# Split first-block weights in the arena, and two units of the second block ahead of the second tile, in a four-sublayer decoder trunk

## The chip, the cores and the metric

One core of one Trainium2 chip runs the whole program. The metric is the device time of one execution in microseconds (us), lower is better.

## The reference

A trunk of two layers over x of 256 tokens by 1024 channels, all in float32. Each layer has a token mixer and then an MLP, so there are four sub-layers, numbered v = 0 to 3 below. Each is normed, modulated and gated, with shift, scale and gate computed from a conditioning vector c:

```python
def trunk(x, c):
    c_act = silu(c)
    for i in range(2):
        sh1, sc1, g1, sh2, sc2, g2 = split(c_act @ ada_w[i] + ada_b[i], 6)
        h = rms_norm(x, norm_mix_g[i]) * (1 + sc1) + sh1
        y = gla_mixer(h) if i == 0 else moba_mixer(h, positions)
        x = x + g1 * y
        h = rms_norm(x, norm_mlp_g[i]) * (1 + sc2) + sh2
        x = x + g2 * (square(relu(h @ mlp_w1[i])) @ mlp_w2[i])    # 1024 -> 4096 -> 1024
    return x
```

v = 0 is gated linear attention (chunks of 64 tokens, 4 heads), v = 2 is block-sparse softmax attention (8 heads of 128, QK norm and rotary on q and k; with 256 tokens there is one block, so it is plain causal attention), v = 1 and 3 are the MLPs.

## The kernel before

**Weights.** Every weight matrix is read from memory once, in units of 128 partitions x 1024 values (two row groups of 128 by 512 columns). SP loads two units with one DMA of 1 MB into one of 4 slots of `w_raw`. A product in float32 is made of three matmuls in fp32r: ACT writes the rounded high part of a unit to `w_hi` (`hi`, L985), DVE writes the remainder to `w_lo` (`lo`, L1342), and PE adds hi x hi, hi x lo and lo x hi (`three`, L479 to L481). `w_hi` and `w_lo` have 4 slots each, so `hi` of unit u waits until PE has finished unit u - 4 (`unit_used`). A slot of `w_raw` is loaded again when `lo` of both its units is done (`lo_made`). Activations are split in the same way: `a_hi` (L1052) on ACT, `a_lo` (L1493) on DVE.

**Blocks.** Four units are a block, 1024 rows by 512 columns. Tokens are in two tiles (tb = 0, 1) of 128. In a token-major block (`project`, `project_tiles`) the activations are the stationary operand and the weights stream 512 columns: 6 matmuls for a unit and a tile. In a channel-major block of an MLP (`up`, L638 to L640) the weights are stationary and 256 tokens stream: 24 matmuls for a unit. Each MLP has 8 pairs of blocks: the hidden block j (up) and its product with w2 (`down`). Hidden block 0 is token-major and is then turned by 8 transposes (`turn`, L623). Hidden blocks 1 to 7 are channel-major, and PE works on hidden block j + 1 before `down` of block j.

**Between two sub-layers.** The last product of a sub-layer ends with tile 0 ahead of tile 1. For each tile: DVE adds the gated result to x (`residual`, L1504 and L1505, two halves of 512 columns), ACT takes squares and the root (`squares`, L1007 to L1015), DVE scales (`scaled`, L1415 to L1419, writes `xn`), PE transposes `xn` (`turn_norm`, L569), and then in four quarters ACT modulates (L1048) and writes `a_hi` (L1052), and DVE writes `a_lo` (L1493). PE needs quarter u of a tile for unit u. The transposes of tile 0 stand before the last unit of the product before; those of tile 1 stand after the four tile-0 units of the next block 0 (`project_tiles`), and then come the four tile-1 units. `norm(v)`, on ACT and on DVE, holds this work in a fixed order, with `hi` and `lo` of the block's own four units in between. The order on every engine is written out by hand; an engine waits in order.

**The block-sparse stage** (v = 2) has 6 input blocks n (k, q, k, q, v, v) and 2 output blocks. On ACT `stats(n)` reads the result of block n out of PSUM (L1095) and takes squares per head (L1192). On DVE `cosines`, `rotate` and `scale` (L1641 to L1667) turn and norm it, one after each of the first three units of block n + 1. PE transposes the result (`turn_rot(n)`, L846) after the first unit of block n + 2. `tables()` (L1817, L1818) makes the rotary tables from `gains`, and `gate1()` adds the last gates (PE L560, DVE L1396).

**ada.** The modulation weights come by the queue of POOL (L359), 1 MB each. `ada()` on DVE multiplies them in (L1357, L1360, two instructions of 128 x 1024), at hand-placed points of the stages up to the first MLP, and twice plus twice at the start of the second.

**The arena** is one buffer of 14.5 K values per partition that the stages share by hand: `xn` at 0, `hT` at 2 K, relu and squares from 4 K to 6 K, the products of attention above.

## Time and profile before

| | us |
|---|---|
| median of 3 runs | 658.9 (656.29 to 660.45) |
| the profiled execution: its own time | 658.67 |
| its span, first to last instruction | 656.9 |
| PE busy in the span | 619.4 (94%) |
| PE weight loads busy | 517.4 (79%) |
| DVE busy | 474.5 (72%) |
| ACT busy | 340.7 (52%) |

The span is what the trace shows; 1.8 us of the execution's own time lie around it. Times of rows count from the start of the span. Matmuls overlap, and the end of each is modelled, so the distance from one matmul's start to the next says more than its duration, and PE counts as busy over very short gaps.

### The profile page before, as it was taken

What the parts mean: (1) busy time and instruction counts of PE and PEld (TensorE: products, weight loads), DVE (VectorE), ACT (ScalarE), POOL (GpSimd) and SP (SyncE); (2) the same over time, 40 slices, a digit from 0 to 9 for tenths busy, and PEclk for the clock granted to TensorE, in tenths of its full rate; (3) what the DMA queues carried; (4) which work ended last, traced back from release to release, by engine and by line L of the source; (5) the groups of instructions that cost most, each with busy time, mean ns of one, the idle gap of its engine ahead of it and who ended that gap; (6) DMA issues with size and microseconds to landing.
All of it is one profiled execution on the core that took longest, in us unless ns stands there. A gap on an engine that the chain in (4) does not pass through costs nothing.

```text
span 656.9 us, 9237 instructions
## 1 busy us (share of the span) xinstructions
PE 619.4 (94%) x3471; PEld 517.4 (79%) x3471; DVE 474.5 (72%) x660; ACT 340.7 (52%) x581; POOL 39.4 (6%) x65
## 2 busy tenths in 40 slices
PE   3699999898999999999997999999799999999997
PEld 2467865676889998998865778788598999899985
DVE  4648997987778978889866987865787654555465
ACT  3446633547755344435548677564875443554440
POOL 3030021000000110101100000000000000000000
PEclk9799999999999999999998999999999999999999
DMA  8999599574588998999955545344357555555501
GB/s 289 387 364 389 166 362 383 215 254 155 175 312 323 378 360 314 340 366 354 341 222 187 175 151 188 133 129 129 128 180 274 188 192 192 192 192 192 192 0 64
DMA packets 58797, 156.44 MB, mean 238 GB/s; under 512 B 2786, under 2 KB 3280, under 8 KB 58768
## 3 DMA queue, kind: packets, MB, share of 16 engines
q1 hardware_dynamic: 47008, 112.41, 48.5%
q0 software_dynamic: 11760, 43.67, 18.6%
q8 instruction: 16, 0.26, 0.2%
q14 instruction: 13, 0.11, 0.0%
HBM read 155.02 MB, written 1.05 MB: 238 GB/s over the span
## 4 chain that ended last, share of the span: by engine, by line
PE 71%; DVE 10%; ACT 7%; issue 3%; ACTq 0%; DVEq 0%
PE ps L479 14%; PE ps L481 13%; PE ps L480 13%; PE ps L640 8%; PE ps L639 8%; PE ps L638 8%; DVE w_lo L1342 2%; ACT arena L1048 2%; ACT w_hi L985 1%; DVE ada_acc L1360 1%; ACT arena L1007 1%; PE ps L560 1%; DVE arena L1419 1%; ACT arena L1192 1%; DVE x L1505 1%
## 5 line engine op out<-in xcount | busy, mean ns | idle before, releaser
L1342 DVE TENSOR_TENSOR w_lo<-w_raw,w_hi 128x1024 fp32r<-128x1024 f32 x192 | 232.8, 1222 | 122.5 <-ACT w_hi L985 122.1
L985 ACT ACTIVATE w_hi<-w_raw 128x1024 fp32r<-128x1024 f32 x192 | 201.8, 1058 | 226.7 <-PE ps L481 119.6
L479 PE MATMUL ps<-w_hi,a_hi 128*128 128x512 f32 x288 | 120.2, 417 | 16.0 <-DVE a_lo L1493 14.3
L638 PE MATMUL ps<-a_hi,w_hi 128*128 128x256 f32 x448 | 126.9, 283 | 0.0
L640 PE MATMUL ps<-a_hi,w_lo 128*128 128x256 f32 x448 | 126.8, 283 | 0.0
L639 PE MATMUL ps<-a_lo,w_hi 128*128 128x256 f32 x448 | 126.7, 283 | 0.0
L481 PE MATMUL ps<-w_hi,a_lo 128*128 128x512 f32 x288 | 114.1, 396 | 0.0
L480 PE MATMUL ps<-w_lo,a_hi 128*128 128x512 f32 x288 | 113.7, 395 | 0.0
L479 PE MATMUL ps<-w_hi,m_hi 128*128 128x512 f32 x256 | 100.1, 391 | 0.0
L480 PE MATMUL ps<-w_lo,m_hi 128*128 128x512 f32 x256 | 99.8, 390 | 0.0
L481 PE MATMUL ps<-w_hi,m_lo 128*128 128x512 f32 x256 | 99.6, 389 | 0.0
L639 PEld LDWEIGHTS ps<-a_lo,w_hi 128*128 128x128 f32 x448 | 85.9, 192 | 0.6
L638 PEld LDWEIGHTS ps<-a_hi,w_hi 128*128 128x128 f32 x448 | 85.9, 192 | 0.5
L640 PEld LDWEIGHTS ps<-a_hi,w_lo 128*128 128x128 f32 x448 | 85.9, 192 | 0.0
L479 PEld LDWEIGHTS ps<-w_hi,a_hi 128*128 128x128 f32 x288 | 55.0, 191 | 38.2 <-issue 12.4
L1360 DVE SCALAR_TENSOR_TENSOR ada_acc<-ada_raw,c_act,ada_acc 128x1024 f32<-128x1024 f32 x56 | 71.7, 1281 | 2.9 <-DMA ada_raw<-in_ada_w_dram 1.7
L481 PEld LDWEIGHTS ps<-w_hi,a_lo 128*128 128x128 f32 x288 | 54.9, 191 | 12.2
L480 PEld LDWEIGHTS ps<-w_lo,a_hi 128*128 128x128 f32 x288 | 55.2, 192 | 10.4 <-issue 0.2
L479 PEld LDWEIGHTS ps<-w_hi,m_hi 128*128 128x128 f32 x256 | 48.1, 188 | 11.0 <-DVE w_lo L1342 0.8
L481 PEld LDWEIGHTS ps<-w_hi,m_lo 128*128 128x128 f32 x256 | 48.1, 188 | 10.2
L480 PEld LDWEIGHTS ps<-w_lo,m_hi 128*128 128x128 f32 x256 | 48.1, 188 | 9.3
L359 POOL DMA_DIRECT2D ada_raw<-in_ada_w_dram x40 | 28.2, 704 | 423.6 <-DVE ada_acc L1360 378.4
(187 smaller groups left out, 506.4 us busy)
## 6 DMA issues: line engine op xcount, KB each, us to landing
w_raw<-in_mlp_w_dram SPq DMA_DIRECT2D x64, 1024.0 KB, 5.6
ada_raw<-in_ada_w_dram POOLq DMA_DIRECT2D x40, 1024.0 KB, 6.3
w_raw<-in_gla_w_in_dram SPq DMA_DIRECT2D x12, 1024.0 KB, 15.7
w_raw<-in_moba_w_in_dram SPq DMA_DIRECT2D x12, 1024.0 KB, 6.3
ada_raw<-in_ada_w_dram SPq DMA_DIRECT2D x4, 1024.0 KB, 12.5
arena<-in_ada_w_dram SPq DMA_DIRECT2D x4, 1024.0 KB, 14.1
w_raw<-in_gla_w_out_dram SPq DMA_DIRECT2D x4, 1024.0 KB, 8.6
w_raw<-in_moba_w_out_dram SPq DMA_DIRECT2D x4, 1024.0 KB, 5.0
```

The costliest lines, as they stand in the source:

```text
L359: nc.gpsimd.dma_start(ada_pair(s), src.rearrange("(k p) n -> p k n", p=P)).then_inc(ada_sw_in[s % 2], 16)
L479: mm(out, hi, w_hi[:, slot, wc], start=first, stop=False)
L480: mm(out, hi, w_lo[:, slot, wc], start=False, stop=False)
L481: return mm(out, lo, w_hi[:, slot, wc], start=False, stop=last)
L560: mm(ps[:, bank, :], ones[:, :], ada_acc[:, acc_slot(b)], start=True, stop=True).then_inc(gate_p, 1)
L638: mm(o, w_hi[:, u, w], a_hi[:, a, :], start=u == 0 and k == 0, stop=False)
L639: mm(o, w_hi[:, u, w], a_lo[:, a, :], start=False, stop=False)
L640: z = mm(o, w_lo[:, u, w], a_hi[:, a, :], start=False, stop=u == 3 and k == 1)
L985: A(w_hi[:, c % SPLIT], w_raw[:, c // 2, c % 2], ACT.Copy).then_inc(hi_made, 1)
L1048: z = A(hT[:, k, ts], ps[:, bank, at + ts.start:at + ts.stop], ACT.Identity, scale=modc[:, l, 2 * s + 1, k:k + 1], bias=modc[:, l, 2 * s, ...
L1342: V.tensor_tensor(w_lo[:, c % SPLIT], w_raw[:, c // 2, c % 2], w_hi[:, c % SPLIT].bitcast(F32), ALU.subtract).then_inc(lo_made, 1)
L1360: z = V.scalar_tensor_tensor(acc, w, c, acc, op0=ALU.mult, op1=ALU.add)
```

## The change

1. **Room.** The arena from 4 K to 14 K becomes also `spare`, 10 units. For the first blocks of v = 1, 2 and 3, `unit_hi` and `unit_lo` give places for four split units there instead of in `w_hi` and `w_lo`. `hi` and `lo` of these units then wait for the last user of that part of the arena, not for `unit_used`. `mod_row` and `gains` move to other places of the arena.
2. **Earlier splits.** `spare_units(v)` on ACT makes the four high parts at the end of the sub-layer before; DVE makes the four low parts between the residuals and around `scaled` of tile 0. `norm(v)` now makes units 4 to 7, into `w_hi` and `w_lo`: 4 and 5 around tile 0, 6 and 7 around tile 1.
3. **PE's order** in these stages is `two_blocks`: block 0 tile 0 (4 units), block 1 tile 0 units 0 and 1 with the transposes of tile 1 between them, block 0 tile 1 (4 units), then the rest of block 1. Before, block 1 began after all of block 0.
4. **MLPs.** Hidden block 1 is token-major too, written to PSUM banks 2 and 3, and needs its own `turn` (8 more transposes in each MLP, in the first `down` after its unit 0), `second_relus` into `relu_2`, and squares by `first_squares(1)`. PE waits for these squares before its loop.
5. **Residuals** of tile 1 are both in `norm(v)`, with `a_lo` of a quarter between the two instructions of each (`between`).
6. **Block-sparse stage.** `gate1` on DVE goes from (0, 3) to after `cosines(0)`; on PE it follows unit 1 of block 1. ACT's `stats(1)` waits for `tables()`.
7. **First norm.** ACT modulates quarter 2 before `hi` of unit 4; DVE makes `lo` of unit 4 after the mods and `a_lo` of quarter 2, not before them.
8. **Output.** Four DMAs of 256 KB, one for each tile and half, in place of two of 512 KB.

```diff
@@ arena
-        arena = sb("arena", [P, ARENA])
+        with nc.sbuf_tensor("arena", [P, ARENA], F32) as arena:
+            pass
+        sb("arena_head", [P, 4 * K1])
+        spare = sb("spare", [P, 10, UNIT], F32R)
+        sb("arena_tail", [P, ARENA - 14 * K1])
+        relu_2 = area(2 * K1, TB, COLS)
-        gains = area(7 * K1, 2, HD)
+        gains = area(12 * K1 + 512, 2, HD)
-        mod_row = area(10 * K1, 2, COLS)
+        mod_row = area(2 * K1, 2, COLS)
+        spare_hi = {v: spare[:, (0 if v == 2 else 2):(4 if v == 2 else 6)] for v in (1, 2, 3)}
+        spare_lo = {v: spare[:, (4 if v == 2 else 6):(8 if v == 2 else 10)] for v in (1, 2, 3)}
+        STAGE_UNIT = {mlp_base[0]: 1, mix_base[1]: 2, mlp_base[1]: 3}
+        def spare_stage(u):
+            return STAGE_UNIT.get(u - u % 4) if isinstance(u, int) else None
@@ SP
-                sp.wait_ge(x_new, x_done(1, 1, 1))
+                sp.wait_ge(unit_used, mlp_base[0] + 4)
...
-                sp.wait_ge(x_new, x_done(2 * DEPTH, tb, 1))
-                sp.dma_start(out_d[0, tb * P:(tb + 1) * P, :], x[:, tb]).then_inc(out_sem, 16)
+                for half in range(2):
+                    cs = slice(half * COLS, (half + 1) * COLS)
+                    sp.wait_ge(x_new, x_done(2 * DEPTH, tb, half))
+                    sp.dma_start(out_d[0, tb * P:(tb + 1) * P, cs], x[:, tb, cs]).then_inc(out_sem, 16)
@@ PE
+            def spare_unit(v, u0, u, bank, tb):
+                for k in range(2):
+                    z = spare_three(ps[:, bank, :], 2 * u + k, tb, u0 + u, slice(k * COLS, (k + 1) * COLS),
+                                    u == 0 and k == 0, u == 3 and k == 1)
+                return z
+            def two_blocks(v, u0, banks, side):
+                for u in range(4):
+                    pe.wait_ge(lo_made, u0 + u + 1)
+                    pe.wait_ge(a_ok, A_NORM[v] + u + 1)
+                    spare_unit(v, u0, u, banks[0], 0)
+                pe.wait_ge(x_new, x_done(v, 1, 1))
+                for u in range(2):
+                    pe.wait_ge(lo_made, u0 + 4 + u + 1)
+                    spare_unit(v, u0 + 4, u, banks[2], 0)
+                    if u == 0:
+                        turn_norm(v, 1)
+                for u in range(4):
+                    pe.wait_ge(a_ok, A_NORM[v] + 4 + u + 1)
+                    spare_unit(v, u0, u, banks[1], 1).then_inc(unit_used, 1)
+                for u in range(4):
+                    if u >= 2:
+                        pe.wait_ge(lo_made, u0 + 4 + u + 1)
+                        spare_unit(v, u0 + 4, u, banks[2], 0)
+                    spare_unit(v, u0 + 4, u, banks[3], 1).then_inc(unit_used, 1)
+                    if u in side:
+                        side[u]()
@@ PE mlp
-                project_tiles(base, (0, 1), A_NORM[v], {(0, 3): lambda: turn_norm(v, 1)})
-                up(base + 4, {1: turn}, first=True)
+                two_blocks(v, base, (0, 1, 2, 3), {1: lambda: turn(0)})
                 pe.wait_ge(sq_ok, 2 * m0 + 2)
-                down(base + 8, 0, True)
+                down(base + 8, 0, True, {0: lambda: turn(1)})
+                pe.wait_ge(sq_ok, 2 * m0 + 4)
@@ PE moba
+                two_blocks(2, mix_base[1], [in_bank(n, tb) for n in range(2) for tb in range(TB)], {1: gate1})
@@ ACT hi
+                v = spare_stage(u)
+                if v == 1:
+                    act.wait_ge(o_p, 2)
+                elif v == 2:
+                    act.wait_ge(m_ok, 2 * NJ)
+                elif v == 3:
+                    act.wait_ge(s_p, MH)
+                    if c % 4 >= 2:
+                        act.wait_ge(oT_ok, 8)
+                elif isinstance(u, int) and spare_stage(u - 4):
+                    act.wait_ge(unit_used, u - 2 * SPLIT + 1)
@@ ACT norm
                 squares(v, 0)
-                for u in range(2):
+                for u in range(4, 6):
                     hi_at(u0 + u)
-                for q in range(2):
-                    modulate_tile(v, 0, (q,))
-                    if q == 0:
-                        hi_at(u0 + 2)
-                modulate_tile(v, 0, (2, 3))
-                hi_at(u0 + 3)
+                modulate_tile(v, 0, range(4))
                 squares(v, 1)
+                for u in range(6, 8):
+                    hi_at(u0 + u)
                 modulate_tile(v, 1, range(4))
@@ DVE norm
+                if v == 3:
+                    spare_units(3, (2,))
                 scaled(v, 0)
-                for u in range(2):
-                    lo_at(u0 + u)
+                spare_units(v, (2, 3) if v == 1 else (3,))
                 low(0, 0)
-                lo_at(u0 + 2)
-                low(0, 1)
                 dve.wait_ge(unit_used, u0)
-                residual(1 - s, 1 - s, 1 if v == 1 else 0, 1)
+                residual(1 - s, 1 - s, 0, 1, lambda: low(0, 1))
                 low(0, 2)
-                if v > 1:
-                    residual(1 - s, 1 - s, 1, 1)
-                lo_at(u0 + 3)
-                low(0, 3)
+                residual(1 - s, 1 - s, 1, 1, lambda: low(0, 3))
+                lo_at(u0 + 4)
                 scaled(v, 1)
+                lo_at(u0 + 5)
                 for q in range(4):
                     low(1, q)
+                for u in range(6, 8):
+                    lo_at(u0 + u)
@@ DVE, before v = 1, 2 and 3
-                for tb in range(TB):
-                    residual(0, 0, 0, tb)
+                residual(0, 0, 0, 0)
+                spare_units(1, range(1))
                 dve.wait_ge(y_ok, 1)
                 residual(0, 0, 1, 0)
+                spare_units(1, range(1, 2))
...
+                if l + 1 < DEPTH:
+                    spare_units(2, range(2))
                 dve.wait_ge(gate_ok, 4 * l + 4)
                 for half in range(2):
                     dve.wait_ge(y_ok, 4 * l + 2 + half)
@@ 
                         for i in (2, 3):
                             mods(2 * l + i, i)
+                        spare_units(2, (2,))
...
+                spare_units(3, range(2))
                 for half in range(2):
                     dve.wait_ge(y_ok, 4 + half)
                     residual(0, 0, half, 0)
@@ DVE mlp
-                for u in range(4):
-                    lo_at(base + 4 + u)
-                    if u in (1, 3):
-                        ada()
+                for _ in range(2):
+                    ada()
```

## Rows read from the trace of the kernel before

**Rows 1.** Busy time by stretch: length, PE, PEld, DVE, ACT, POOL, granted clock, DMA share, GB/s

```profile
153.00:167.00 14.00, 10.63 (x47) 7.24 (x46) 8.70 (x16) 11.48 (x29) 0.00 (x0) 1.00 0.43 150
200.00:322.00 122.00, 122.00 (x789) 111.87 (x788) 105.27 (x105) 57.70 (x68) 13.52 (x20) 1.00 0.94 350
```

**Rows 2.** Who waited for whom: us in total, times, longest

```profile
PE ps L479 <- DVE a_lo L1493: 14.3, 12, 3.3
```

**Rows 3.** PE from the second tile of v = 1: start, us, what

```profile
165.67 0.50 PE L479 MATMUL ps<-w_hi,a_hi 128*128 128x512 f32 x1 [1.43 <-DVE a_lo L1493]
...
171.25 0.28 PE L638 MATMUL ps<-a_hi,w_hi 128*128 128x256 f32 x1
...
177.01 1.04 PE L623 MATMUL ps<-eye,arena 128*128 128x128 f32 x8
177.80 0.36 PE L638 MATMUL ps<-a_hi,w_hi 128*128 128x256 f32 x1
...
183.63 0.40 PE L479 MATMUL ps<-w_hi,m_hi 128*128 128x512 f32 x1
```

**Rows 4.** PE at the second tile of v = 2 and of v = 3

```profile
357.16 0.50 PE L479 MATMUL ps<-w_hi,a_hi 128*128 128x512 f32 x1 [1.43 <-DVE a_lo L1493]
...
476.07 0.50 PE L479 MATMUL ps<-w_hi,a_hi 128*128 128x512 f32 x1 [1.43 <-DVE a_lo L1493]
```

**Rows 5.** Groups of instructions: count, busy us, mean ns, idle time before

```profile
L1342 DVE TENSOR_TENSOR w_lo<-w_raw,w_hi 128x1024 fp32r<-128x1024 f32 x192 | 232.8, 1222 | 122.5 <-ACT w_hi L985 122.1
L985 ACT ACTIVATE w_hi<-w_raw 128x1024 fp32r<-128x1024 f32 x192 | 201.8, 1058 | 226.7 <-PE ps L481 119.6 <-PE ps L640 99.7 <-DMA w_raw<-in_gla_w_in_dram 7.5
L1493 DVE TENSOR_TENSOR a_lo<-arena,a_hi 128x256 fp32r<-128x256 f32 (+1 forms) x28 | 12.9, 461 | 13.1 <-ACT a_hi L1052 12.8 <-ACT a_hi L1031 0.3
```

**Rows 6.** ACT, modulation of two quarters of the second tile of v = 1

```profile
163.90 0.81 ACT L1048 ACTIVATE arena<-ps,modc 128x128 f32<-128x128 f32 x2 [2.17 <-PE ps L569]
...
165.06 0.79 ACT L1048 ACTIVATE arena<-ps,modc 128x128 f32<-128x128 f32 x2
```

**Rows 7.** DVE in v = 1: `scaled` of tile 0, `lo` of unit 3, `scaled` of tile 1

```profile
151.28 0.81 DVE L1419 TENSOR_SCALAR arena<-x,stat 128x1024 f32<-128x1024 f32 x1
...
159.59 1.23 DVE L1342 TENSOR_TENSOR w_lo<-w_raw,w_hi 128x1024 fp32r<-128x1024 f32 x1 [1.16 <-ACT w_hi L985]
...
162.28 0.81 DVE L1419 TENSOR_SCALAR arena<-x,stat 128x1024 f32<-128x1024 f32 x1
```

**Rows 8.** DVE before v = 2: the second residual of tile 0

```profile
339.40 0.69 DVE L1504 TENSOR_TENSOR arena<-ps,gates 128x512 f32<-128x512 f32 x1 [1.57 <-PE ps L481]
```

**Rows 9.** ACT in v = 2: `stats(0)` begins, `hi` of unit 8

```profile
365.54 1.07 ACT L1095 ACTIVATE arena<-ps 128x512 f32<-128x512 f32 x2
...
369.56 1.05 ACT L985 ACTIVATE w_hi<-w_raw 128x1024 fp32r<-128x1024 f32 x1
```

**Rows 10.** DVE in v = 2: gates, `lo` of unit 8, `scale(0)`

```profile
368.97 1.29 DVE L1396 TENSOR_TENSOR gates<-ps,gates 128x512 f32<-128x512 f32 x2
370.64 1.23 DVE L1342 TENSOR_TENSOR w_lo<-w_raw,w_hi 128x1024 fp32r<-128x1024 f32 x1 [0.38 <-ACT w_hi L985]
...
379.00 1.23 DVE L1667 TENSOR_TENSOR arena<-arena,stat 128x1024 f32<-128x1024 f32 x1
```

**Rows 11.** PE in v = 2: the first two `turn_rot`

```profile
380.28 1.09 PE L846 MATMUL ps<-eye,arena 128*128 128x128 f32 x8 [0.38 <-DVE arena L1667]
...
392.99 1.09 PE L846 MATMUL ps<-eye,arena 128*128 128x128 f32 x8 [0.72 <-DVE arena L1667]
```

**Rows 12.** PE near the start: first weight matmul after an idle stretch

```profile
25.49 0.77 PE L479 MATMUL ps<-w_hi,a_hi 128*128 128x512 f32 x1 [3.31 <-DVE a_lo L1493]
```

**Rows 13.** Two stretches at a lower granted clock, columns as in Rows 1

```profile
24.00:26.00 2.00, 0.51 (x1) 0.50 (x2) 2.00 (x3) 1.97 (x4) 0.00 (x0) 0.50 1.04 387
...
357.70:361.00 3.30, 3.30 (x9) 2.59 (x8) 1.28 (x3) 3.24 (x8) 0.00 (x0) 0.51 1.04 398
```

**Rows 14.** The output's DMAs: count, size of each, median us from issue to landing

```profile
out_dram<-x SPq DMA_DIRECT2D x2, 512.0 KB, 2.6
```

More of the change, by code:

```diff
@@ L481, in three, with spare_three @@
                 return mm(out, lo, w_hi[:, slot, wc], start=False, stop=last)
+            def spare_three(out, k, tb, u, wc, first, last):
+                hi, lo = a_hi[:, k, tile(tb)], a_lo[:, k, tile(tb)]
+                mm(out, hi, unit_hi(u)[:, wc], start=first, stop=False)
+                mm(out, hi, unit_lo(u)[:, wc], start=False, stop=False)
+                return mm(out, lo, unit_hi(u)[:, wc], start=False, stop=last)
+            def spare_unit(v, u0, u, bank, tb):
[24 more added lines that the diff above has]
+                        side[u]()
             def project(u0, banks, a_wait=None, side={}):
@@ L632, in up @@
                         for c in (2, 3, 0, 1):
-                            if first and u == 0 and c == 0:
-                                pe.wait_ge(relu_ok, 2 * m0 + 2)
                             o = ps[:, c, 0:SEQ]
@@ L641, in up, with down @@
                         z.then_inc(unit_used, 1)
-                        if u in side:
-                            side[u]()
-                def down(u0, j, first):
+                def down(u0, j, first, side={}):
                     for u in range(4):
@@ L1269, in squares_of, with first_squares, second_relus @@
                     A(sq[:, 2 * b:2 * b + 2], src, ACT.Square).then_inc(sq_ok, 1)
-                def first_squares():
+                def first_squares(i):
                     for b in range(2):
-                        act.wait_ge(tr_ok, 2 * l + b + 1)
-                        squares_of(0, b, ps[:, 4 + b, :].rearrange("p (c t) -> p c t", c=2))
+                        act.wait_ge(tr_ok, 4 * l + 2 * i + b + 1)
+                        squares_of(i, b, ps[:, (0 if i else 4) + b, :].rearrange("p (c t) -> p c t", c=2))
+                def second_relus():
+                    act.wait_ge(unit_used, base + 8)
+                    for tb in range(TB):
+                        A(relu_2[:, tb], ps[:, 2 + tb, :], ACT.Relu).then_inc(relu_ok, 1)
                 def hidden(j, u_done):
@@ L1290, in step @@
                         if c == 1 and first:
-                            first_squares()
-                    hidden(j + 1, u0)
+                            first_squares(0)
+                    if first:
+                        second_relus()
+                    else:
+                        hidden(j + 1, u0)
                     if more:
@@ L1295, in step @@
                             hi(u0 + 4 + c, 4 + c, round_)
-                for u in range(4):
-                    hi_at(base + 4 + u)
-                    if u == 2:
-                        relus()
+                            if c == 0 and first:
+                                first_squares(1)
+                relus()
                 step(base + 8, base // 8 + 1, 0, first=True)
@@ L1498, in o_low, with residual @@
                     a_low(A_OUT[l] + q, q, ps[:, 4 + q, :].rearrange("p (c t) -> p c t", c=2), slice(0, SEQ))
-            def residual(mlp_, s, half, tb):
+            def residual(mlp_, s, half, tb, between=None):
                 cs = slice(half * COLS, (half + 1) * COLS)
@@ L1504, in residual @@
                 link(V.tensor_tensor(t, ps[:, y_bank(mlp_, half, tb), :], gates[:, s, cs], ALU.mult))
+                if between is not None:
+                    between()
                 V.tensor_tensor(x[:, tb, cs], x[:, tb, cs], t, ALU.add).then_inc(x_new, 1)
@@ L1700, in follow @@
                         tables()
-                        gate1()
                     for h in range(MH):
@@ L1709, in follow @@
                         (cosines, rotate, scale)[u](n - 1)
+                    if (n, u) == (1, 0):
+                        gate1()
                     for h in range(1, MH, 2):
```

85 lines of the change are left out of this document (53 added, 32 removed).

## The prediction

> **What bounds the kernel now.** The stretches by engine come first. In the loop of the first MLP PE is busy for all of 122 us [rows 1], DVE for 105 of them. The loop is PE's, and what the change gains ahead of it is kept. In the 14 us between GLA and the first MLP, PE is busy for 10.6 us and ACT for 11.5 of 14 [rows 1]; two more stretches like it stand before v = 2 and v = 3. The waits name the cause: PE waits 14.3 us in 12 pieces for `a_lo` of DVE [rows 2]. The third view is PE in order of time: in v = 1, 2 and 3 alike the second tile starts after a last wait of 1.43 us [rows 3, 4]. So the norm chain ends last there: residual, squares, `scaled`, transposes, modulation, `a_lo`. DVE and ACT carry it, and they also split the next block's four units inside it: 1.22 us on DVE and 1.06 on ACT for a unit [rows 5]. One shows itself: `lo` of unit 3 starts at 159.59 after 1.16 us of waiting for its `hi` [rows 7], and `scaled` of tile 1 stands behind it.
>
> **v = 1, worked through.** On the path before, tile 0 is scaled at 151.28 + 0.81 = 152.1 and tile 1 at 163.1 [rows 7]. The new path starts at the same 152.1: one `lo` takes the place of the tile-1 residual that stood there (1.4 us), in front of a residual that waits for PE anyway. From 152.1 DVE has in its order two spare `lo` (2.3), `a_lo` of quarter 0 (0.4), two residual halves of two instructions each at 0.69 to 0.7, one of them in [rows 8], with three `a_lo` between (2.8 + 1.2), `lo` of unit 4 (1.15), and the statistics with `scaled` (0.6 + 0.8). This is 9.3 us. ACT's quarters are 1.16 us apart [rows 6] and are now uninterrupted, so they end at 157.7 and hold DVE back by some 0.2. Tile 1 is scaled at about 161.6, 1.5 us earlier. The transposes end at 162.4, ACT's `hi` of units 6 and 7 ends at 162.2 just before, and one modulation with its `a_lo` is 1.8 us, 163.90 to 165.67 [rows 3, 6]. The second tile starts at 164.3, against 165.67 [rows 3].
>
> Two units of block 1 lie ahead of it. A tile and a unit is 1.38 us, from (171.25 - 165.67) / 4 = 1.40 with its slow first matmul. Is there room? Four units run from 154.9 to 160.3, unit 4 to 161.7 (its `lo` at 160.0), then the transposes, and unit 5 from 162.8 to 164.2 (its `lo` at 162.7). They fill what was idle, and PE is free just as quarter 0 of the second tile is ready.
>
> From the second tile to `down` there are then 4 + 6 tile-units and a turn: 10 x 1.38 + 0.8 = 14.6 us, so `down` starts at 178.9. Before it is 183.63 [rows 3], a gain of 4.7. The second turn costs 8 transposes, 0.8 us (177.01 to 177.80) [rows 3] plus a restart: 0.85. Net for v = 1: **3.9 us**. Block 1 as token-major saves 0.7 of this by the rows (12.38 less 0.8 is 11.6 us for 96 matmuls of 256 columns; 8 x 1.365 = 10.9 for 48 of 512). I bound it by 0 and 0.9.
>
> A rule speaks against that last term. The Trainium skill (TensorE: Matmul & The Clock Gate, Back-to-back issue gap) gives an isolated gap of N / 2.4 + 2.5 ns, by which 96 matmuls of 256 columns are 10.5 us and 48 of 512 are 10.4. By it the sum over two MLPs would be 1.2 us less. The trace has 0.120 us for 256 columns where the page has 0.109, and so I stay with the rows.
>
> New waits inside the MLP: `down` needs hidden block 0 split on DVE. After `norm` DVE has two `lo`, two `ada()` in a row (4.6 us), two `lo` and `hidden(0)`, and I find 178.7 for its last part against PE's 178.9. This is just hidden; each us that DVE is later is a us of PE. ACT's `second_relus` follows `hi` of unit 11 and ends about 0.4 us before PE's second turn. The wait for squares before the loop has 8 us of `down` over it. The loop is as before, at 94% DMA share [rows 1]; its loads now start 4 us earlier with earlier `lo`, so I cost nothing, with up to 2 us if the DMAs do not follow.
>
> **v = 3** is the same with one difference. The two spare `lo` on DVE stand ahead of the residuals and delay them by 0.35 us. The second tile starts at 475.0 against 476.07 [rows 4]. Net **3.6 us**.
>
> **v = 2.** Two spare `lo` and a third stand ahead of the second residual of tile 0, which had been waiting for PE until 339.40 [rows 8]; I find 339.9, 0.5 us later. The same steps as above then give a second tile at 356.2 against 357.16 [rows 4]. Before, its first matmuls ran at 1.2 GHz: the granted clock is 0.51 from 357.70 to 361.00 [rows 13], which cost 1.7 us. With less idle time ahead of it I take it to be gone. Block 1 would end at 371.2, 5.6 us earlier than the 376.8 that I read off before.
>
> But this does not reach the end. `turn_rot(0)` follows the next unit, at 374.0, and it waits for `scale(0)`, a chain of ACT and DVE that was already late by 0.38 and 0.72 us for the first two turns [rows 11]. `stats(0)` can start when tile 1 of block 0 ends, 362.0 instead of 365.54; it takes 4.0 us to `hi` of unit 8 [rows 9]. From there to `lo` of unit 8 it is 1.1 and to the end of `scale(0)` 9.6 (370.64 to 380.23) [rows 10]. `gate1` (1.29 us, 1.2 in a row) [rows 10], once ahead of this, now lies inside it. 362.0 + 4.0 + 1.1 + 9.6 + 1.2 = 377.9, against 380.23. PE stands still from 374.0 to 377.9. At `turn_rot(1)` the same chain, now tied to PE by `hi` of unit 13, gives 390.1 against 392.99 [rows 11]: a gain of 2.9 us that is kept, since the later blocks stand in the same balance.
>
> The clock decides the rest. PE ran at half clock at 25.49 after 3.31 us without work [rows 12, 13], and it fell once more after the shorter waits of v = 2, but not after those of v = 1 and 3. A whole gap of 3.9 us is nearest to the first of these rows, so I take a fall to 1.2 GHz. It lasts some 3.3 to 4.5 us after PE resumes (the first from [rows 13], the second my reading of the start), at half of that lost: 1.9 us, all of it on the chain of `turn_rot(1)` through units 9 and 10. Net for v = 2: **1.0 us**; 2.9 without the fall. No row excludes a little less than nothing, so its bounds are -1 and 3.
>
> **Small ones.** The output: 512 KB land 2.6 us after issue [rows 14], and the last DMA has now 256 KB; I take 0.4 us off, between 0 and 0.8. (The Trainium skill, DMA: Bandwidth & Descriptors, Anatomy of one DMA, has a fixed cost of about 2.0 us in a DMA. By it halving the bytes takes off 0.3; the trace has no second size of output.) The first norm: `lo` of unit 4 no longer holds back the mods, and PE gets quarter 2 some 1.2 us earlier. The stage then hangs on DVE's own order, which starts over when the next weights arrive, whatever PE does. I take 0, with 1.2 above. The wait of `stats(1)` for the tables (ready at 364.5, wanted at 372) and SP's new wait for `gains` cost nothing: both have 7 us of other work over them.
>
> **The sum**, against the profiled execution's own 658.67 us: 3.9 + 3.6 + 1.0 + 0.4 = 8.9, which gives **649.8 us**. The median of the runs, 658.9, is 0.2 above it, within what runs differ, and I leave the number.
>
> **Rivals.**
> (a) The clock does not fall in the gap of v = 2: 8.9 + 1.9 = 10.8, 647.9 us. For it: twice of three times it held through waits that add up to as much. Against it: none of those waits was in one piece.
> (b) The two units ahead are not free. DVE gets `lo` of units 4 and 5 in between the norm's own steps; where DVE, not ACT, is late there, the second tile starts where it did and PE only moves two units about. For it: my times for `lo` of unit 5 and for unit 5 are 0.1 us apart. Against it: DVE loses four `lo` from the same stretch. Then v = 1 and 3 give some 2 us each, v = 2 none: 654.5 us.
> (c) Slower: the gap in v = 2 repeats at every `turn_rot`, and the clock stays at 1.2 GHz through the block-sparse stage (PE works through nearly all of it). Each us at half clock costs 0.5, so it decides from 18 us of half clock on, and eats the gain at that point; with 40 us it is 658.67 - 8.9 + 20 = 670. Against it: the first two turns are 12.7 us apart [rows 11] and PE has 11.8 us of work between them (4 x 2.73 and a turn), so only the first gap is long.
> (d) The change does not do what it says: the new splits wait for the arena (for the second MLP `s_p` and `oT_ok`, for v = 2 the last `m_lo`) and come as late as before. By the trace each of these is past by the time ACT is free, with 5 us at least of idle ACT ahead of each norm. It would give 657.
>
> **How the numbers follow.** A measurement of this kernel tells about 1% (6.6 us) from no change. My forecast 0.45, (a) 0.22, (b) 0.22, (c) 0.03, (d) 0.05, and 0.03 for a still larger gain. The range is from 646.5 ((a) with the first norm's 1.2) to 654.7 ((b) and a late DVE in the MLPs). Faster by over 1% is below 652.1: the forecast and (a) with nearly all of their width, part of (b), 0.75. Within 1%: most of (b) and (d), 0.21. Slower: 0.04.
>
> **What the profile after would show.** Right: in v = 1 and v = 3 PE has no wait over 0.6 us between the two transposes and `down`, and 8 transposes more; the second tile starts 1 to 1.5 us earlier relative to `scaled` of tile 0; before the first `turn_rot` PE idles 3 to 4 us for `scale(0)` (L1667 before), followed by a granted clock near 0.5. Wrong: waits of PE for `w_lo` at units 4 and 5 (rival b); a wait for `m_lo` at the first `down`; a clock of 1.00 through v = 2 (rival a); or DVE waiting for loads in the first MLP. The prediction would fail most easily on DVE's order around `scaled`, where I count to 0.1 us.

## The result

| | before | after |
|---|---|---|
| median, us | 658.7 (656.29 to 660.45, 4 runs) | 649.6 (647.2 to 651.25, 4 runs) |
| ratio to before, 95% interval | | 0.9856 [0.9825, 0.9888] |
| span of the profiled execution, us | 656.9 | 649.5 |

The kernel is 9.1 us faster (1.4%; by the interval between 7.4 and 11.5 us). The forecast was 649.8.

Each of the three norms begins with eight transposes of its first tile; call their start T0. Distances from T0 to T0 cut the span into stretches that can be compared between traces. The last row of the table is the time from T0 of v = 3 to the end of the span.

| us | before | after | gain |
|---|---|---|---|
| start to T0 of v = 1 | 152.24 | 153.53 | -1.29 |
| T0 of v = 1 to T0 of v = 2 | 191.47 | 188.44 | 3.03 |
| T0 of v = 2 to T0 of v = 3 | 118.89 | 117.47 | 1.42 |
| T0 of v = 3 to the end | 194.3 | 190.06 | 4.24 |

From T0 of v = 1 on the gain is 8.69 us. The first stretch belongs to the execution: in three traces of the changed kernel it is 153.53, 151.42 and 153.55 us, while the other stretches repeat within 0.2 us (experiments 4 and 12).

**v = 1.** PE of the changed kernel in order of time: the two sets of norm transposes with unit 5 of the weights behind the second, then the turn and the first matmul of `down`.

```profile
153.53 1.07 PE L631 MATMUL ps<-eye,arena 128*128 128x128 f32 x8 [0.27 <-DVE arena L1509]
...
163.23 1.04 PE L631 MATMUL ps<-eye,arena 128*128 128x128 f32 x8
164.03 0.50 PE L510 MATMUL ps<-w_hi,a_hi 128*128 128x512 f32 x1
...
174.15 1.03 PE L685 MATMUL ps<-eye,arena 128*128 128x128 f32 x8
...
180.49 0.39 PE L503 MATMUL ps<-w_hi,m_hi 128*128 128x512 f32 x1
```

The wait of 1.43 us of [rows 3] is gone: unit 5 follows the transposes at once, and the second tile starts 12.16 us after T0, before 13.43. `down` starts 26.96 us after T0; before it was 183.63 - 152.24 = 31.39, so 4.4 us are won up to there. The waits, in the view that names who waited for whom (us in total, times, longest):

```profile
PEld ps L906 <- DVE arena L1764: 5.7, 3, 3.7
PE ps L503 <- DVE a_lo L1587: 5.1, 2, 3.3
PE ps L906 <- DVE arena L1764: 4.4, 3, 3.3
```

PE waited 14.3 us in 12 pieces for `a_lo` [rows 2]; 5.1 in 2 are left, and 3.3 of these are the wait at the kernel's start. In the norms PE no longer waits for it. What has grown is the wait for `scale(n)`, 4.4 us with 3.3 in one piece; in the kernel before it was:

```profile
PE ps L846 <- DVE arena L1667: 1.5, 3, 0.7
```

DVE at the second tile of v = 1 shows how close unit 5 is to its low part:

```profile
160.01 1.22 DVE L1433 TENSOR_TENSOR w_lo<-w_raw,w_hi 128x1024 fp32r<-128x1024 f32 x1
...
162.03 0.81 DVE L1509 TENSOR_SCALAR arena<-x,stat 128x1024 f32<-128x1024 f32 x1
162.75 1.22 DVE L1433 TENSOR_TENSOR w_lo<-w_raw,w_hi 128x1024 fp32r<-128x1024 f32 x1
```

`lo` of unit 5 begins at 162.75 and unit 5 starts on PE at 164.03: the `lo` of 1.22 us ends when the transposes do, so nothing is to spare and nothing is lost.

**v = 2.** PE around the first `turn_rot`:

```profile
372.28 0.39 PE L505 MATMUL ps<-w_hi,a_lo 128*128 128x512 f32 x1
375.99 1.97 PE L906 MATMUL ps<-eye,arena 128*128 128x128 f32 x8 [3.33 <-DVE arena L1764]
377.61 0.78 PE L503 MATMUL ps<-w_hi,a_hi 128*128 128x512 f32 x1
378.18 0.63 PE L504 MATMUL ps<-w_lo,a_hi 128*128 128x512 f32 x1
378.61 0.49 PE L505 MATMUL ps<-w_hi,a_lo 128*128 128x512 f32 x1
378.94 0.39 PE L503 MATMUL ps<-w_hi,a_hi 128*128 128x512 f32 x1
```

PE stands for 3.33 us, and the eight transposes then take 1.97 us, where they took 1.09 [rows 11]. The stretches give the clock (length, busy time of PE, PEld, DVE, ACT, POOL, granted clock, DMA share, GB/s):

```profile
374.00:376.00 2.00, 0.01 (x1) 0.01 (x1) 1.86 (x6) 1.94 (x7) 0.00 (x0) 0.85 0.18 67
376.00:378.00 2.00, 2.00 (x9) 2.00 (x10) 2.00 (x2) 0.09 (x2) 0.00 (x0) 0.50 0.00 0
378.00:379.00 1.00, 1.00 (x4) 0.77 (x4) 1.00 (x3) 1.00 (x2) 0.00 (x0) 0.59 0.78 127
379.00:380.00 1.00, 1.00 (x6) 0.83 (x5) 0.41 (x1) 0.08 (x1) 0.00 (x0) 1.00 0.99 350
```

The clock is at its lower level, 1.2 GHz, from about 375.4, still inside the wait, to about 378.8. Ahead of this gap, from 341 to 372, it is 1.00: the 1.7 us at half clock of [rows 13] did not come again. DVE in the same stretch has `gate1` between `cosines(0)` and the next `lo`, and `scale(0)` as the last step of an unbroken sequence:

```profile
365.16 1.23 DVE L1433 TENSOR_TENSOR w_lo<-w_raw,w_hi 128x1024 fp32r<-128x1024 f32 x1 [3.22 <-ACT w_hi L1051]
366.30 1.29 DVE L1738 TENSOR_TENSOR arena<-arena 128x512 f32<-128x512 f32 x2
367.50 1.28 DVE L1486 TENSOR_TENSOR gates<-ps,gates 128x512 f32<-128x512 f32 x2
...
374.71 1.23 DVE L1764 TENSOR_TENSOR arena<-arena,stat 128x1024 f32<-128x1024 f32 x1
```

### The profile page after: what moved, and what is told of

It reads as the page before. It is cut to its first block, busy times and chain, and to the rows that moved or that the text cites. A ratio compares the mean times of both kernels' runs of the same rounds, so it can differ in the third digit from the quotient of the medians.

```text
span 649.5 us, 9093 instructions
## 1 busy us (share of the span) xinstructions
PE 621.5 (96%) x3391; PEld 516.6 (80%) x3391; DVE 474.5 (73%) x660; ACT 341.0 (53%) x581; POOL 39.4 (6%) x65
## 4 chain that ended last, share of the span: by engine, by line
PE 78%; DVE 12%; ACT 4%; issue 3%; DMA 2%; SPq 0%; DVEq 0%; ACTq 0%
PE ps L503 13%; PE ps L504 13%; PE ps L505 13%; PE ps L700 7%; PE ps L699 7%; PE ps L698 7%; PE ps L510 3%; PE ps L512 3%; PE ps L511 3%; DVE w_lo L1433 2%; DMA arena<-in_ada_w_dram 2%; DVE spare L1433 1%; PE ps L607 1%; DVE ada_acc L1450 1%; PE ps L615 1%
## 5 line engine op out<-in xcount | busy, mean ns | idle before, releaser
L1051 ACT ACTIVATE w_hi<-w_raw 128x1024 fp32r<-128x1024 f32 x180 | 189.1, 1058 | 215.4 <-PE ps L505 117.7
L1433 DVE TENSOR_TENSOR w_lo<-w_raw,w_hi 128x1024 fp32r<-128x1024 f32 x180 | 218.3, 1222 | 109.5 <-ACT w_hi L1051 109.3
L700 PE MATMUL ps<-a_hi,w_lo 128*128 128x256 f32 x384 | 108.7, 283 | 0.0
L699 PE MATMUL ps<-a_lo,w_hi 128*128 128x256 f32 x384 | 108.7, 283 | 0.0
L698 PE MATMUL ps<-a_hi,w_hi 128*128 128x256 f32 x384 | 108.6, 283 | 0.0
L503 PE MATMUL ps<-w_hi,a_hi 128*128 128x512 f32 x224 | 93.0, 415 | 5.1 <-DVE a_lo L1587 5.1
L504 PE MATMUL ps<-w_lo,a_hi 128*128 128x512 f32 x224 | 88.6, 396 | 0.0
L505 PE MATMUL ps<-w_hi,a_lo 128*128 128x512 f32 x224 | 88.6, 396 | 0.0
L699 PEld LDWEIGHTS ps<-a_lo,w_hi 128*128 128x128 f32 x384 | 73.7, 192 | 0.5
L503 PEld LDWEIGHTS ps<-w_hi,m_hi 128*128 128x128 f32 x256 | 48.1, 188 | 11.1 <-DVE w_lo L1433 0.8
L504 PEld LDWEIGHTS ps<-w_lo,a_hi 128*128 128x128 f32 x224 | 42.9, 191 | 8.1
```

The source lines that it names most:

```text
L503: mm(out, hi, w_hi[:, slot, wc], start=first, stop=False)
L504: mm(out, hi, w_lo[:, slot, wc], start=False, stop=False)
L505: return mm(out, lo, w_hi[:, slot, wc], start=False, stop=last)
L698: mm(o, w_hi[:, u, w], a_hi[:, a, :], start=u == 0 and k == 0, stop=False)
L699: mm(o, w_hi[:, u, w], a_lo[:, a, :], start=False, stop=False)
L700: z = mm(o, w_lo[:, u, w], a_hi[:, a, :], start=False, stop=u == 3 and k == 1)
```

## The experiments

Two groups of questions. Were the gains in v = 1 and 3 from the early splits and the units ahead (experiments 1, 2 and 9)? And was v = 2 really held by the chain to `scale(0)`, and is its cure in reach (3, 5, 6, 7, 10)? Two more repeat the changed kernel (4, 12) and one undoes the part that I had costed at nothing (8).

All by stretches, in us. Columns "first" and "second `turn_rot`" count from T0 of v = 2.

| | T0 v=1 to v=2 | first | second | T0 v=2 to v=3 | T0 v=3 to end | median |
|---|---|---|---|---|---|---|
| before | 191.47 | 36.57 | 49.28 | 118.89 | 194.3 | 658.7 |
| after | 188.44 | 34.02 | 47.62 | 117.47 | 190.06 | 649.6 |
| 1 none ahead | 190.72 | 33.77 | 46.23 | 116.12 | 192.61 | 654.05 |
| 2 late `lo` | 191.72 | 37.65 | 51.50 | 121.17 | 193.99 | 659.06 |
| 3 none ahead, v = 2 | 188.27 | 33.78 | 46.26 | 116.12 | 190.09 | 648.81 |
| 4 after again | 188.23 | 34.00 | 47.56 | 117.44 | 190.11 | 649.76 |
| 5 `gate1` early | 188.24 | 32.79 | 46.66 | 116.53 | 190.07 | 648.46 |
| 6 turn later | 188.32 | 33.98 | 44.60 | 114.42 | 190.13 | 646.58 |
| 7 both | 188.24 | 33.21 | 43.72 | 113.59 | 190.08 | 644.84 |
| 8 first norm | 188.24 | 33.98 | 47.88 | 117.76 | 190.03 | 649.16 |
| 9 channel-major | 190.39 | 33.75 | 46.21 | 116.08 | 192.28 | 652.24 |
| 10 both, none ahead, v = 2 | 188.25 | 35.71 | 46.24 | 116.13 | 190.05 | 647.73 |
| 11 both again | 188.25 | 33.25 | 43.77 | 113.68 | 190.03 | 645.44 |
| 12 after, third | 188.24 | 34.00 | 47.76 | 117.61 | 190.1 | 650.05 |

1 to 4 ran on one chip, 5 to 8 on one, 9 to 12 on one; the kernel before had 656.64, 658.48 and 657.62 us there. The changed kernel itself did not run beside 5 to 8, so these are read by their stretches, which repeat within 0.2 us in its three traces.

**1. No unit ahead of the second tile.**

```diff
+                ahead = 0 if True else 2
                 pe.wait_ge(x_new, x_done(v, 1, 1))
-                for u in range(2):
+                if not ahead:
+                    turn_norm(v, 1)
+                for u in range(ahead):
...
-                    if u >= 2:
+                    if u >= ahead:
```

> Split units and hidden block 1 as in the changed kernel, but PE takes no unit of block 1 ahead of the second tile in v = 1, 2 and 3: it goes from the transposes of tile 1 straight to block 0 tile 1. My theory: the two units ahead are free in v = 1 and v = 3 because they lie in PE's idle time; without them the second tile starts where it did, PE waits some 2.7 us more ahead of it, and down starts 2.7 us later; v = 2 gives nothing, since its first turn_rot waits for scale(0) anyway. 649.6 + 5.4 = 655.0 us. Rival (b), the units ahead only move work about: the second tile starts earlier by as much as they took, and the time stays at 649.6. If PE is the slower for more idle time (the granted clock falls ahead of the second tile, as it did in v = 2 of the kernel before), up to 1.7 us more in each of the three.

Measured 654.05 us (653.42 to 655.12), 4.3 above the changed kernel beside it. By stretches v = 1 and v = 3 lose 2.49 and 2.50 us, and v = 2 gains 1.3, which the expectation had left out (experiment 3 explains it). The wait ahead of the second tile is back as it was, in v = 1 and then in v = 2:

```profile
165.62 0.50 PE L510 MATMUL ps<-spare,a_hi 128*128 128x512 f32 x1 [1.43 <-DVE a_lo L1590]
...
353.87 1.06 PE L634 MATMUL ps<-eye,arena 128*128 128x128 f32 x8 [0.96 <-issue]
356.36 0.50 PE L510 MATMUL ps<-spare,a_hi 128*128 128x512 f32 x1 [1.43 <-DVE a_lo L1590]
```

The second tile of v = 1 starts 11.87 us after T0, with the units ahead 12.16. So the two units, 2.75 us of PE, cost the second tile 0.3 and are otherwise free: rival (b) falls for v = 1 and 3. `down` starts 29.40 us after T0, 2.44 later than with them.

**2. All spare `lo` inside the norm.**

```diff
-                if v == 3:
-                    spare_units(3, (2,))
                 scaled(v, 0)
-                spare_units(v, (2, 3) if v == 1 else (3,))
+                spare_units(v)
...
-                spare_units(1, range(1))
...
-                spare_units(1, range(1, 2))
...
-                spare_units(3, range(2))
...
-                if l + 1 < DEPTH:
-                    spare_units(2, range(2))
...
-                        spare_units(2, (2,))
```

> As the changed kernel, but DVE makes all four spare lo of v = 1, 2 and 3 inside the norm, after scaled of tile 0, and none around the residuals before it. My theory: DVE is what carries the norm, so each lo that comes back into it (1.15 us) moves scaled of tile 1 and with it the second tile: v = 1 has two back (2.3 us), v = 2 and v = 3 have three (3.4 us), less 0.5 in v = 2 and 0.35 in v = 3 by which the residuals of tile 0 come earlier. The units ahead cover none of it, for lo of units 4 and 5 moves too. v = 1 and 3 cost 2.3 + 3.1 = 5.4 us; v = 2 moves stats(0) and the chain to scale(0) by 2.9. Together 649.6 + 8.3 = 657.9 us. Rival: ACT's quarters, not DVE, end last, or the units ahead cover the wait: within 1 us of 649.6.

Measured 659.06 us (654.84 to 661.68), 9.3 more than the changed kernel; the stretches of the traced execution say 3.5 + 3.7 + 3.9 = 11.1. All the gain of the change is lost by the place of eight instructions of DVE. The direction is that of my theory and the size is 3 us over it, but the way is another: four `lo` in a row hold back `a_lo` of quarter 0 of the first tile, and PE waits for it in one piece in all three norms, 2.42, 2.42 and 2.50 us. PE in v = 1, with the transposes of tile 1 behind, and DVE's `scaled` of tile 1:

```profile
156.59 0.62 PE L510 MATMUL ps<-spare,a_hi 128*128 128x512 f32 x1 [2.42 <-DVE a_lo L1585]
...
165.20 1.03 PE L631 MATMUL ps<-eye,arena 128*128 128x128 f32 x8
```

```profile
162.04 0.81 DVE L1509 TENSOR_SCALAR arena<-x,stat 128x1024 f32<-128x1024 f32 x1
```

The stretches after the wait show the granted clock:

```profile
156.00:158.00 2.00, 1.41 (x4) 1.14 (x5) 1.97 (x5) 1.11 (x3) 0.00 (x0) 0.69 1.02 418
158.00:160.00 2.00, 2.00 (x7) 1.52 (x5) 1.97 (x5) 1.02 (x3) 0.00 (x0) 0.50 1.02 412
160.00:162.00 2.00, 2.00 (x10) 1.63 (x9) 1.74 (x5) 1.73 (x5) 0.00 (x0) 0.96 0.41 164
```

PE fell to 1.2 GHz, and so it did in v = 2 (0.58 from 348 to 352) and v = 3 (0.60 from 470 to 474). In v = 1 it lasts from 156.59 to about 160, half of which is 1.7 us; I had counted DVE's `lo`, and neither this wait nor the clock after it. DVE itself is late by a little less than I had: from `scaled` of tile 0 to that of tile 1 it takes 11.28 us, against 9.43 in experiment 4, 1.85 more and not 2.3. But this no longer decides: `scaled` of tile 1 is done at 162.9, the transposes start at 165.20 without a wait, 3.8 us later from T0 than in experiment 4, and so it is PE's own order behind the first tile that sets the second one. The kernel before had the four `lo` spread between the `a_lo`, two, one and one. So this experiment shows what a bad place costs, and not what the early splits gave; experiment 9 is nearer to that.

**3. No unit ahead in v = 2 alone**: as in 1, with `ahead = 0 if v == 2 else 2`.

> As the changed kernel, but in v = 2 alone PE takes no unit of block 1 ahead of the second tile. My theory: the chain stats(0), hi of unit 8, lo of unit 8, scale(0) sets the first turn_rot, and it starts with the end of block 0 tile 1, which is not moved; so the units ahead bring nothing here, the 3.3 us wait before the first turn_rot shrinks to 0.6, and the time is that of the changed kernel, 649.6 us within 0.5; if the granted clock then does not fall after the first turn_rot, 1.3 us less, 648.3. Rival: the wait moves ahead of the second tile and the clock falls there as in the kernel before: 1.7 us at half clock ahead of stats(0), so 651.3 less the 1.3 of the other fall, 650.0. Rival (b) in this stage (the two units are a gain of 2.7 us there too): 652.3.

Measured 648.81 us (647.23 to 650.99), 0.95 less than the changed kernel beside it, which the medians alone do not settle; the stretch has 1.3 less. The first two `turn_rot`:

```profile
374.27 1.09 PE L909 MATMUL ps<-eye,arena 128*128 128x128 f32 x8 [0.61 <-DVE arena L1767]
...
386.75 1.09 PE L909 MATMUL ps<-eye,arena 128*128 128x128 f32 x8 [0.48 <-DVE arena L1767]
```

The wait is 0.61 in place of 3.33, the transposes are back at 1.09 us and the clock is 1.00 from T0 of v = 2 to 380. The first `turn_rot` comes at the same place (33.78 against 34.0): it hangs on the chain alone. The second comes 1.3 us earlier. Of this 1.1 lie between the two turns, where PE has the same work (12.48 us against 13.56 in experiment 4): that is the price of the half clock, and the other 0.2 is the chain's earlier end. In v = 2 the part of the change that gives 2.5 us elsewhere gives nothing and costs 1.3.

**4 and 12. The changed kernel again.**

> The changed kernel once more, on the chip of the other three, so that each stands against it there: 649.6 us, ratio 0.986 to the kernel before. All theories expect the same; a second trace also tells what of its start (the granted clock of 0.79 in the first 40 us) belongs to a run and not to the kernel.

> The changed kernel a third time, as the base of e10 and e11 on their chip: 649.7 us, ratio to the kernel before 0.9856 to 0.9905, as the first two measurements had it. All theories expect the same.

649.76 us with ratio 0.9905 [0.9886, 0.9925], and 650.05 with 0.9869 [0.9836, 0.9902]. The time of the changed kernel repeats within 0.5 us. The first of the two ratios is higher since the kernel before was at 656.64 there.

**5. DVE's `gate1` ahead of `cosines(0)`.**

```diff
                     if (n, u) == (0, 3):
                         tables()
+                        gate1()
...
-                    if (n, u) == (1, 0):
-                        gate1()
```

> As the changed kernel, but gate1 of DVE (1.28 us) is back ahead of cosines(0), after the tables, where DVE is idle for 3.2 us; PE's place for it stays. My theory: gate1 lies in the chain from stats(0) to scale(0), which alone sets the first turn_rot. That turn_rot comes 1.2 us earlier, PE's wait before it falls from 3.3 to 2.1 us, and the time is 649.7 - 1.2 = 648.5 us, or 647.2 if the granted clock no longer falls after the shorter wait. Rival: the chain is held by ACT (stats(0), hi of units 8 to 11), gate1 fits into a wait of DVE for hi, and nothing changes, 649.7.

Measured 648.46 us (648.17 to 649.86). DVE now does it where it was idle:

```profile
362.79 0.69 DVE L1486 TENSOR_TENSOR gates<-ps,gates 128x512 f32<-128x512 f32 x1 [1.76 <-PE ps L622]
363.65 0.69 DVE L1486 TENSOR_TENSOR gates<-ps,gates 128x512 f32<-128x512 f32 x1 [0.17 <-PE ps L622]
```

and the first `turn_rot` is 1.2 us earlier, after a wait of 2.14 us:

```profile
373.89 1.49 PE L906 MATMUL ps<-eye,arena 128*128 128x128 f32 x8 [2.14 <-DVE arena L1764]
```

`gate1` was in the chain, and the rival falls. The clock fell all the same (0.56 from 374.0 to 377.5). The stretch keeps 0.9 us; the median is 0.7 under that of experiment 8 on the same chip, and the two ranges overlap.

**6. The first `turn_rot` one unit later**, on PE, and its read on ACT:

```diff
-                    if u == 0 and 2 <= n < 6:
+                    if (n, u) in ((2, 1), (3, 0), (4, 0), (5, 0)):
                         turn_rot(n - 2)
```

> As the changed kernel, but the first turn_rot (and ACT's read of it) comes one unit later, after unit (2, 1) and not (2, 0). My theory: scale(0) ends when it did, and PE has 2.7 us of work to do meanwhile; its wait falls from 3.3 to 0.6 us, the clock stays at 1.00 (1.3 us), and lo of unit 13, for which DVE waits 2.9 us because PE must first use unit 9, comes at once. scale(1) is then 2.9 us earlier: 646.9 us, with about 1.4 us of a new wait before the second turn_rot. Rival: the chain on DVE is fixed by its own work from scale(0) on, the wait only moves to the second turn_rot, and only the clock is won: 648.4.

Measured 646.58 us (645.58 to 646.87).

```profile
374.43 1.09 PE L906 MATMUL ps<-eye,arena 128*128 128x128 f32 x8 [0.62 <-DVE arena L1764]
...
385.05 1.09 PE L906 MATMUL ps<-eye,arena 128*128 128x128 f32 x8 [1.35 <-DVE arena L1764]
```

`scale(0)` is where it was (33.98), PE waits 0.62, then 1.35 at the second turn, the clock is 1.00 from 340 to 400, and the second turn is 3.0 us earlier. The order of PE fed back into the chain through `hi` of unit 13, which waits for PE to use unit 9. DVE's `lo` of unit 13, in the changed kernel and then here:

```profile
382.30 1.23 DVE L1433 TENSOR_TENSOR w_lo<-w_raw,w_hi 128x1024 fp32r<-128x1024 f32 x1 [2.89 <-ACT w_hi L1051]
```

```profile
377.77 1.22 DVE L1433 TENSOR_TENSOR w_lo<-w_raw,w_hi 128x1024 fp32r<-128x1024 f32 x1
```

The wait of 2.89 us is gone; the rival, in which the chain runs on by itself, falls.

**7 and 11. Both.**

> e5 and e6 together: gate1 of DVE ahead of cosines(0), first turn_rot one unit later. My theory: scale(0) is ready (1.2 us earlier) before unit (2, 1) ends, PE has no wait before the first turn_rot, the clock stays, and scale(1) follows 1.2 us earlier than in e6 alone: 645.7 us, the best of all. Rival: either cure alone is enough and the two together give no more than the better of them, 646.9.

> e7 once more, on one chip with the changed kernel: 644.8 us, 4.8 us less than the changed kernel (1.3 from the clock, 1.2 from gate1, the rest from PE's work in the place of its wait). Rival: part of the difference between e7 and the changed kernel was the chip, 646.5.

644.84 us (644.62 to 645.68), ratio 0.9794 [0.977, 0.9817], and again 645.44 us (644.67 to 646.52), 4.6 below the changed kernel on its chip. PE has no wait before the first turn, and 1.29 before the second, and the clock is again 1.00 from 340 to 400:

```profile
373.44 1.03 PE L906 MATMUL ps<-eye,arena 128*128 128x128 f32 x8
...
383.95 1.09 PE L906 MATMUL ps<-eye,arena 128*128 128x128 f32 x8 [1.29 <-DVE arena L1764]
```

It beats both kernels: 13.6 us under the one before in the first measurement, 12.2 in the second.

**8. The first norm as before**: `hi` of units 4 and 5 ahead of the modulation of quarters 2 and 3 on ACT, `lo` of unit 4 ahead of the modulations on DVE.

```diff
-                for q in range(2, 4):
-                    modulate(0, slice(0, SEQ), 0, (q,))
-                    hi_at(2 + q)
+                for u in range(4, 6):
+                    hi_at(u)
+                modulate(0, slice(0, SEQ), 0, range(2, 4))
...
+                lo_at(4)
                 for i in range(2, 4):
                     first_mods(i, ADA_FIRST[i], i - 2)
-                modulate(0, slice(0, SEQ), 0, 0, range(2, 4), lambda q: lo_at(4) if q == 3 else None)
-                for u in range(5, 8):
+                modulate(0, slice(0, SEQ), 0, 0, range(2, 4), lambda q: lo_at(5) if q == 3 else None)
+                for u in range(6, 8):
```

> As the changed kernel, but part 7 of the change is undone: in the first norm ACT splits units 4 and 5 ahead of the modulation of quarters 2 and 3, and DVE makes lo of unit 4 ahead of the modulations. I costed this part at nothing: 649.7 us. Rival: quarter 2 comes some 1.2 us later to PE and the delay is kept, 650.9 us; most of it would show as a wait of PE before unit (0, 2).

Measured 649.16 us (648.33 to 651.32), no slower than the three medians of the changed kernel (649.6 to 650.05). From the first weight matmul to T0 of v = 1 it is 124.96 us, against 124.65, 124.49 and 124.71. Whatever this part gives is some 0.3 us at most; four other kernels with the new first norm and a start as late (first weight matmul from 27.9 us on) have 124.41 to 124.90.

**9. Hidden block 1 channel-major**, without units ahead, to be read against 1.

```diff
-                two_blocks(v, base, (0, 1, 2, 3), {1: lambda: turn(0)})
+                two_blocks(v, base, (0, 1, 2, 3), {})
+                up(base + 4, {1: lambda: turn(0)}, first=True)
                 pe.wait_ge(sq_ok, 2 * m0 + 2)
-                down(base + 8, 0, True, {0: lambda: turn(1)})
-                pe.wait_ge(sq_ok, 2 * m0 + 4)
+                down(base + 8, 0, True)
```

`two_blocks` stops after block 0 in the MLPs here, and ACT takes squares and relus of hidden block 1 as in the kernel before.

> As e1 (no unit of block 1 ahead of the second tile in v = 1, 2 and 3, splits as in the changed kernel), but hidden block 1 of both MLPs is channel-major as in the kernel before: 96 matmuls of 256 columns each, no second turn. It prices the layout alone. By the rows (12.38 - 0.8 against 8 x 1.365, and a second turn of 0.85) channel-major is 0.15 us faster in each MLP: 653.8 against 654.05 us of e1, and the same ratio within 0.001. Rival, the rule of the Trainium skill (TensorE: Matmul & The Clock Gate, Back-to-back issue gap), an estimate: 10.5 against 10.4 us of matmuls, so that the second turn is all loss and channel-major is 0.75 us faster in each MLP, 652.5 us.

Measured 652.24 us (651.86 to 653.15). This is nearer to the rival's 652.5 than to the 653.8 that I expected, but 1 ran on another chip, so the stretches decide. Those of v = 1 and v = 3 are both 0.33 us shorter than in 1, 0.66 together (of the 1.8 us between the two spans 1.1 lie before T0 of v = 1): more than the 0.15 that I had for each, less than the rival's 0.75. From the second tile to `down` it is 183.15 - 165.62 = 17.53 us in 1 and 182.62 - 164.53 = 18.09 here, so the token-major layout saves 0.56 us of matmuls; the second turn costs 185.88 to 186.66 and a restart, 0.87. It is a small loss, which the layout has to pay so that its units can go ahead of the second tile (2.5 us). The estimate from the Trainium skill (TensorE: Matmul & The Clock Gate, Back-to-back issue gap), by which nearly nothing is saved, does not hold here: matmuls of 256 columns were 0.120 us apart where it gives 0.109.

```profile
172.52 0.28 PE L696 MATMUL ps<-a_lo,w_hi 128*128 128x256 f32 x1
172.64 0.28 PE L697 MATMUL ps<-a_hi,w_lo 128*128 128x256 f32 x1
```

This kernel has the layout of the one before and no unit ahead, but the early splits and the new order of the norm. So the times from T0 to `down` in v = 1 price the parts of the change: 31.39 before, 29.97 here, 29.40 in 1 with the token-major block, 26.96 in the changed kernel with the units ahead. That is 1.4, 0.6 and 2.4 us; the second turn, 0.87, comes behind and is to be taken off. How the 1.4 divide between the splits and the rest of the norm's order stays open; no experiment has one without the other.

**10. Experiment 7 without units ahead in v = 2.**

> e7 (gate1 of DVE early, first turn_rot after unit (2, 1)), but PE takes no unit of block 1 ahead of the second tile in v = 2. In the changed kernel those two units bought nothing in v = 2, since the chain to scale(0) ended last. My theory: in e7 that chain no longer ends last, PE does, so now they do count. The first turn_rot comes 2.5 us later than in e7; the second, which waits 1.3 us for scale(1) in e7, comes 1.2 us later: 644.8 + 1.2 = 646.0 us, up to 647.3 if that wait stays. Rival: the units ahead are worth nothing in v = 2 in any case, 644.8.

Measured 647.73 us (647.61 to 649.59), 2.3 above 11 beside it. The first turn is at 35.71 from T0, as expected. The second is 2.5 us later than in 7, not 1.2:

```profile
387.86 1.09 PE L909 MATMUL ps<-eye,arena 128*128 128x128 f32 x8 [1.30 <-DVE arena L1767]
```

The wait of 1.3 us stays, since `stats(1)` starts when PE ends block 1 (31.44 us after T0, 28.97 in 11), and so the second chain moves with PE. Once the first chain no longer ends last, the two units ahead are worth 2.5 us in v = 2 as well.

## Why the prediction was right

The total was right and so was each larger term of it, by its own mechanism. That it came within 0.2 us is in part luck: the ratio's interval alone is 4 us wide, and in v = 2 two sizes were off and cancel.

**v = 1, 3.9 us: 3.6.** The second tile was forecast 12.06 us after T0 and came at 12.16; `down` at 26.66 and came at 26.96. That is 4.43 us, less 0.87 of the second turn, 3.56. The other 0.5 of the stretch (3.03) is by subtraction the later T0 of v = 2, which I had entered there at 0.5; PE's wait before that T0 grew from 0.27 to 0.61 us. The part taken from the layout was 0.56 where I took 0.7. `down` did not wait for `m_lo`: it ends at about 180.2, 0.3 ahead of PE; the margin that I had at 0.2 held.

**v = 3, 3.6 us: 3.4** (4.24 less the output's 0.6 and less 0.26, by which PE's wait before T0 of v = 3 grew, 0.44 against 0.18; I had 0.35 for it).

**v = 2, 1.0 us: 1.15** (1.42 less the 0.5 above, and with the 0.26 that belongs to v = 3). The wait before the first `turn_rot` was 3.33 us, not 3.9, since PE itself came later to it. The fall of the clock cost 1.1 to 1.3 us, not 1.9 (experiment 3): I counted from the moment when PE resumes 3.3 to 4.5 us at half clock, and it was 2.8, as the clock had been down for a part of the wait already. Against that, without the fall the second turn is 3.0 us earlier from T0, where I had 2.9 after taking off the 0.5 of T0, that is 3.4. `gate1` inside the chain is as I had it (1.21 against 1.2, experiment 5).

**Output, 0.4: 0.6.** The DMAs of 256 KB land 2.0 us after issue, against 2.6 for 512 KB [rows 14]. The second figure that I had beside the 0.4, 0.3, is half of that. An estimate from the two sizes: 0.6 us for 256 KB, and 2.0 - 0.6 = 1.4 us that do not shrink with the bytes.

```profile
out_dram<-x SPq DMA_DIRECT2D x4, 256.0 KB, 2.0
```

**First norm, 0: some 0.3 at most** (experiment 8). **The first loads of the loop**, costed at nothing: v = 1's stretch accounts for all of its gain, so they cost nothing.

Sum: 3.56 + 3.37 + 1.15 + 0.61 = 8.7, forecast 8.9. Two figures beside the sum are off by 0.2: by its own terms (b) comes to 654.3 and not 654.5, and the lower end of the range to 646.7 and not 646.5.

**The rivals.** (a) did not occur; had it, it would be worth some 1.3 us, as experiment 3 has it. (b) holds in v = 2 alone, for a reason that is not that of the rival: not DVE's `lo` but the chain behind block 0 ends last. (c) The first gap is the only long one: the later turns wait 0.27 and 0.81 us and the clock stays at 1.00 there. (d) The spare parts come in time in all three stages. What I did not see, though the rows had it, is that the gap of v = 2 could be filled from both sides by moving two calls, which is worth half of what the whole change gave.

## What to carry to other kernels

When a stage is held by a chain on other engines, take freely placed work out of that chain (here, with the new order of the norm, 1.4 us a stage), and give the idle engine work from the next block (2.5 us a stage). What is left must not stand in a row ahead of the chain's first result: four `lo` there cost 9 to 11 us over three stages. Then look at once for what is late next: the same two units brought nothing in v = 2 until one call of DVE and one turn of PE had been moved. From the first MLP on, each wait of TensorE of 2.14 to 3.34 us in one piece had the half clock behind it; price such a wait with that, 1.1 to 1.3 us where it was taken out.

## What was not expected of the hardware

**The clock and short waits.** After waits of 2.14, 2.42, 2.50 and 3.3 us in one piece, from the first MLP on, the clock was at 1.2 GHz each time. After one of 1.77 us, at 128 us in the changed kernel, it was at 1.00, and so it was in all 14 traces. With two waits of 0.96 and 1.43 us within 3.5 us it held in the three stages of experiment 1, the three of 9 and in v = 2 of 3 and 10; in experiment 3 with PE busy for 1.06 of 3 us:

```profile
349.00:352.00 3.00, 1.06 (x8) 0.85 (x8) 2.02 (x3) 2.67 (x6) 0.00 (x0) 1.00 0.95 280
```

In v = 2 of the kernel before it did fall after such pieces [rows 13], and not in its v = 1 and 3. What tells these apart stays open.

**The start.** Before its first full transposes, at 8.2 to 8.8 us, PE stands for some 5 us in every trace, and they still run at 1.00. The clock then falls once ahead of the first weight matmul, and when it does so differs from one execution to the next: it is low from 23.2 to 30.1 us before, and from 17.0 to 34.1, 18.0 to 31.7 and 17.1 to 34.2 in traces of the changed kernel. The forecast took the 3.31 us without work of [rows 12] for the cause of such a fall. In that trace the wait does begin 1.0 us before the fall, but in those three the clock was low 5.6 to 8.6 us before the same wait began. The first weight matmul came at 25.49 us before, and in traces of the changed kernel at 28.88, 26.93 and 28.84; T0 of v = 1 differs by 2.1 us among the three. That is more than several of the parts of this change, and a reason to compare stretches from a fixed event and not spans.
